# A decoder step's wkv stage: merge levels as one 64x64 matmul per head, and engine loops written out

## The reference, cut to what matters

```python
def step(S, inp):
    r_t, d_t, k_t, v_t, a_t, b_t = inp
    Sa = jnp.einsum('bhvk,bhk->bhv', S, a_t)
    S = S * d_t[:, :, None, :] + Sa[..., :, None] * b_t[..., None, :] + v_t[..., :, None] * k_t[..., None, :]
    return S, jnp.einsum('bhvk,bhk->bhv', S, r_t)
S, ys = lax.scan(step, S0, xs)
```

## Time and profile before

| | |
|---|---|
| median of 3 runs | 4897.39 us (4886.02 to 4908.73) |
| profiled execution, first to last instruction | 4900.2 us |
| mean granted TensorE clock | 0.914 |
| TensorE matmuls | busy 4308.0 us (88%) |
| VectorE | busy 2273.0 us (46%) |
| ScalarE | busy 1456.1 us (30%) |
| GpSimd | busy 1416.4 us (29%) |

### The profile page before, as it was taken

One profiled execution on the slowest core, in us unless ns is written; L12 is line 12 of the kernel. 1 busy time (PEld: TensorE's weight loads), 2 busy tenths in 40 slices (PEclk: granted clock), 3 DMA queues, 4 the chain that ended last, 5 costly groups with the idle time before them and its releaser, 6 DMA issues.

```text
span 4900.2 us, 72602 instructions
## 1 busy us (share of the span) xinstructions
PE 4308.0 (88%) x22425; PEld 3583.0 (73%) x22425; DVE 2273.0 (46%) x4969; ACT 1456.1 (30%) x2858; POOL 1416.4 (29%) x1222
## 2 busy tenths in 40 slices
PE   3789988998889989997989889997989787899996
PEld 3569866886679757885779667885879665678885
DVE  1246534545255535454266535444154553245554
ACT  1333233333333233333323233333322212022222
POOL 6232032443231123442331124442221011023331
PEclk9899998998889999998999899997998888699997
DMA  2320122332310112332310213332210112222221
GB/s 73 125 69 1 43 69 65 94 94 73 103 44 1 60 52 86 94 97 77 88 32 0 78 44 103 94 94 78 64 31 0 52 35 86 90 61 73 68 68 57
DMA packets 454929, 320.54 MB, mean 65 GB/s; under 512 B 18012, under 2 KB 420262, under 8 KB 453070
## 3 DMA queue, kind: packets, MB, share of 16 engines
q1 hardware_dynamic: 454758, 318.45, 21.1%
HBM read 296.99 MB, written 21.61 MB: 65 GB/s over the span
## 4 chain that ended last, share of the span: by engine, by line
PE 68%; DVE 15%; issue 9%; POOL 3%; ACT 3%; DMA 1%; DVEq 1%; ACTq 0%; POOLq 0%; SPq 0%
PE psum L671 66%; DVE xlo L1429 2%; PE psum L675 2%; POOL wlo L577 1%; DVE xT L1429 1%; DVE shifted L1429 1%; DVE zr L1432 1%; DVE ws L1429 1%; ACT whi L1102 1%; DVE shifted L1432 1%; DVE kkn_y L1429 1%; POOL stage L519 1%; DVE xT L1432 0%; DMA out_y_prompt<-zr 0%; ACT stage L1102 0%
## 5 line engine op out<-in xcount | busy, mean ns | idle before, releaser
L577 POOL TENSOR_TENSOR wlo<-wraw,whi 128x1024 fp32r<-128x1024 f32 x480 | 1152.3, 2401 | 2818.6 <-ACT whi L1102 2818.5
L671 PE MATMUL psum<-xhi,whi 128*128 128x512 f32 (+1 forms) x3136 | 1254.3, 400 | 58.5 <-DVE xlo L1429 41.1
L671 PE MATMUL psum<-xhi,wlo 128*128 128x512 f32 (+1 forms) x3136 | 1224.0, 390 | 0.0
L671 PE MATMUL psum<-xlo,whi 128*128 128x512 f32 (+1 forms) x3136 | 1224.0, 390 | 0.0
L1102 ACT ACTIVATE whi<-wraw 128x1024 fp32r<-128x1024 f32 x480 | 507.4, 1057 | 1226.2 <-PE psum L671 1161.4
L671 PEld LDWEIGHTS psum<-xhi,whi 128*128 128x128 f32 x3136 | 599.7, 191 | 231.6 <-DVE xlo L1429 81.1
L671 PEld LDWEIGHTS psum<-xhi,wlo 128*128 128x128 f32 x3136 | 599.7, 191 | 125.0
L671 PEld LDWEIGHTS psum<-xlo,whi 128*128 128x128 f32 x3136 | 601.2, 192 | 113.0 <-issue 1.4
L1429 DVE TENSOR_TENSOR xT<-xT,psum 128x512 f32<-128x512 f32 (+1 forms) x416 | 286.0, 688 | 246.0 <-PE psum L671 166.5
L1741 DVE TENSOR_SCALAR zr<-zr,fcw 128x512 f32<-128x512 f32 x176 | 91.9, 522 | 585.2 <-POOL fcarry L619 583.5
L671 PE MATMUL psum<-ws 128*128 128x64 f32 (+1 forms) x2560 | 350.7, 283 | 2.1 <-DVE ws L1595 1.7
(11 more groups left out here) (292 smaller groups left out, 5587.7 us busy)
## 6 DMA issues: line engine op xcount, KB each, us to landing
wraw<-in_w_up SPq DMA_DIRECT2D x176, 512.0 KB, 3.8
wraw<-in_w_in SPq DMA_DIRECT2D x104, 512.0 KB, 3.9
wraw<-in_w_down SPq DMA_DIRECT2D x88, 512.0 KB, 3.5
wraw<-in_w_out SPq DMA_DIRECT2D x32, 512.0 KB, 4.1
wraw<-in_wq SPq DMA_DIRECT2D x32, 512.0 KB, 4.0
wraw<-in_wo SPq DMA_DIRECT2D x32, 512.0 KB, 4.1
kkn_y<-in_x_prompt SPq DMA_DIRECT2D x4, 2048.0 KB, 9.3
xT_scratch<-xT SPq DMA_DIRECT2D x4, 2048.0 KB, 7.6
```

Of the source, the lines that this page charges most:

```text
L577: return e.tensor_tensor(wlo[i][:, :, :], wraw[i][:, :, :], whi[i][:, :, :].bitcast(F32), ALU.subtract).then_inc(lo_ready[i], 1)
L671: return e.matmul(out, lhsT, rhs, start=start, stop=stop)
```

## The change

1. In the merge levels each product of a pair of heads becomes two, one per head. The weights are the 64x64 diagonal block of the head, the moving side the head's 64 rows and 32 columns, and the result goes to the head's 64 partitions and its own 32 columns of the same bank. The parts of the bank that belong to neither head are no longer written; no copy uses them.
2. Every engine loop (blocks, projections, wkv, FFN and the others, on all engines) is written out as straight code, with constant waits and constant addresses. `LOOPS`, `Counts.loop`, `check_turn` and the increments of `passedA`, `passedG` and `passedV` go.

```diff
+                def per_head(bk, col, lhsT, rhs):
+                    n = 32 // rhs.shape[2]
+                    for h in range(2):
+                        a = slice(64 * h, 64 * h + 64)
+                        ins = mm(psum[a, bk, col + 32 * h:col + 32 * h + 32], lhsT[a, a], rhs[a, n * h:n * (h + 1), :])
+                    return ins
...
-                        mm(psum[:, bk, 0:64], TM[i][:, p, 384:512], half(QT[i][:, p, 0, :], m, 1)).then_inc(wk_mm[bk], 1)
+                        per_head(bk, 0, TM[i][:, p, 384:512], half(QT[i][:, p, 0, :], m, 1)).then_inc(wk_mm[bk], 1)
...
-                        ins = mm(psum[:, bk, 0:64], QT[i][:, p, 1, :], half(Zs[i][:, p, :], m, 1))
+                        ins = per_head(bk, 0, QT[i][:, p, 1, :], half(Zs[i][:, p, :], m, 1))
                         if l < len(MERGES) - 1:
-                            ins = mm(psum[:, bk, 64:128], Zs[i][:, p, :], half(QT[i][:, p, 1, :], m, 0))
+                            ins = per_head(bk, 64, Zs[i][:, p, :], half(QT[i][:, p, 1, :], m, 0))
...
-                with c.loop("wkv", NC // 2 - 1):
+                for _ in range(NC // 2 - 1):
                     wkv_pair()
...
-            with c.loop("block", NB - 1) as b:
+            for b in range(NB - 1):
                 one_block(b, False)
             one_block(NB - 1, True)
...
                 for l in range(1, len(MERGES)):
                     for i, p, bk in both:
                         e.wait_ge(wk_mm[bk], c(wk_mm[bk], 2))
-                        e.sem_inc(passedV, 1)
```

More of the change, by code:

```diff
@@ L1 @@
-from contextlib import ExitStack, contextmanager
+from contextlib import ExitStack
 import numpy as np
@@ L52 @@
 NLD = len(PAR) + 11
[L55 to L141, removed]
@@ L144, with __init__ @@
 class Counts:
-    def __init__(self, eng, name, passed=None):
-        self.eng, self.name, self.passed, self.n, self.turns = eng, name, passed, {}, []
+    def __init__(self):
+        self.n = {}
     def __call__(self, sem, k=1):
         v = self.n[sem.name] = self.n.get(sem.name, 0) + k
-        for i, per in self.turns:
-            if per.get(sem.name):
-                v = i * per[sem.name] + v
         return v
@@ L161, in skip @@
         self.n[sem.name] = self.n.get(sem.name, 0) + k
-    @contextmanager
-    def loop(self, label, count):
-        key = f"{self.name}.{label}"
-        per, before = LOOPS.get(key, {}), dict(self.n)
-        if self.passed is not None and self.turns:
-            self.eng.sem_inc(self.passed, 1)
-        with self.eng.Fori(0, count) as i:
-            self.turns.append((i, per))
-            yield i
-            self.turns.pop()
-        did = {s: v - before.get(s, 0) for s, v in self.n.items() if v != before.get(s, 0)}
-        check_turn(key, per, did)
-        for s, d in did.items():
-            self.n[s] = before.get(s, 0) + d * count
-def check_turn(key, per, did):
-    assert per == did, f"{key}: a turn asks for {did}"
 def hybrid_decoder_step(nc, I, O):
@@ L368, in _ @@
         def _(e):
-            c = Counts(e, "sync")
+            c = Counts()
             def slab(i, src, first=False):
@@ L419, in one_block @@
                 e.dma_start(xT_dram, xT[:, :, :].rearrange("p k t -> p (k t)")).then_inc(x_out, 16)
-                with c.loop("in", NIN // 2 - 1) as i:
+                for i in range(NIN // 2 - 1):
                     for j in range(2):
@@ L429, in one_block @@
                         sample_caches()
-                    with c.loop(name, KT // 2 - 1) as i:
+                    for i in range(KT // 2 - 1):
                         for j in range(2):
@@ L435, in one_block @@
                 ffn_up(0)
-                with c.loop("ffn", NF // 2 - 1) as i:
+                for i in range(NF // 2 - 1):
                     ffn_up(i + 1)
@@ L514, in _ @@
         def _(e):
-            c = Counts(e, "pool", passedG)
+            c = Counts()
             last = [0]
@@ L580, in splits @@
             def splits(label, pairs):
-                with c.loop(label, pairs):
+                for _ in range(pairs):
                     split(0)
@@ L609, in operands @@
                     e.wait_ge(qt_free, c(qt_free))
-                    e.sem_inc(passedG, 1)
                 unit(i)
@@ L639, in one_block @@
                 operands(1, C, True)
-                with c.loop("wkv", NC // 2 - 1) as j:
+                for j in range(NC // 2 - 1):
                     operands(0, j * (2 * C) + 2 * C)
@@ L667, in _ @@
         def _(e):
-            c = Counts(e, "pe")
+            c = Counts()
             def mm(out, lhsT, rhs, start=True, stop=True):
@@ L708, in phase @@
                 if pairs > 1:
-                    with c.loop(label + "s" * bool(sample), pairs - 1):
+                    for _ in range(pairs - 1):
                         dense(0, 0, sample, None, n)
@@ L937, in one_block @@
                 head_rows(8)
-                with c.loop("gates" + "s" * last, 4):
+                for _ in range(4):
                     dense(0, 0, s)
@@ L986, in one_block @@
                 ffn_up(s, tuple(range(KT)))
-                with c.loop("ffn" + "s" * last, NF // 2 - 1):
+                for _ in range(NF // 2 - 1):
                     ffn_up(s)
@@ L1098, in _ @@
         def _(e):
-            c = Counts(e, "act", passedA)
+            c = Counts()
             def act(out, src, func=ACT.Copy, **k):
@@ L1138, in _ @@
                 split_x(k, NMEM)
-            with c.loop("mem", 8):
+            for _ in range(8):
                 for j in range(2):
@@ L1174, in wkv_pair @@
                         e.wait_ge(wk_mm[bk], c(wk_mm[bk], 2))
-                        e.sem_inc(passedA, 1)
                         act(Y[:, p, bass.ds(t0 + i * C, C)], psum[:, bk, 0:C]).then_inc(wk_act[bk], 1)
             def residual(label):
-                with c.loop(label, KT // 2) as i:
+                for i in range(KT // 2):
                     for j in range(2):
@@ L1255, in one_block @@
                     split_x(k)
-                with c.loop("shift", NRW // 2) as i:
+                for i in range(NRW // 2):
                     for j in range(2):
@@ L1287, in one_block @@
                 gate_b(1)
-                with c.loop("gate_c", 2) as i:
+                for i in range(2):
                     for j in range(2):
                         e.wait_ge(slab_done[j], c(slab_done[j]))
-                        e.sem_inc(passedA, 1)
                         act(cb[:, bass.ds(2 * i + j, 1), 2:TB + 2].rearrange("p a t -> p (a t)"), psum[:, j, :]).then_inc(ach, 1)
@@ L1296, in one_block @@
                         split_w(j)
-                with c.loop("h_in", 2):
+                for _ in range(2):
                     for j in range(2):
@@ L1313, in one_block @@
                 dec_chunk(1)
-                with c.loop("wkv", NC // 2 - 1) as i:
+                for i in range(NC // 2 - 1):
                     wkv_pair(i * (2 * C), 2 * i + 2)
@@ L1331, in one_block @@
                     split_x(k)
-                with c.loop("q", KT // 2) as i:
+                for i in range(KT // 2):
                     for j in range(2):
                         e.wait_ge(slab_done[j], c(slab_done[j]))
-                        e.sem_inc(passedA, 1)
                         act(q_sb[:, bass.ds(2 * i + j, 1), :].rearrange("p a t -> p (a t)"), psum[:, j, :]).then_inc(ach, 1)
@@ L1352, in one_block @@
                 ffn_hidden()
-                with c.loop("ffn" + "s" * last, NF // 2 - 1) as i:
+                for i in range(NF // 2 - 1):
                     ffn_up(i + 1)
@@ L1425, in _ @@
         def _(e):
-            c = Counts(e, "dve", passedV)
+            c = Counts()
             def tt(out, a, b, op=ALU.mult):
@@ L1556, in _ @@
             lo(before, NMEM)
-            with c.loop("mem", 8) as i:
+            for i in range(8):
                 for j in range(2):
@@ L1644, in residual @@
                 acc_start()
-                with c.loop(label + "s" * last, KT // 2) as i:
+                for i in range(KT // 2):
                     for j in range(2):
@@ L1830, in sample_out @@
                         e.sem_inc(free[4 + j], 1)
-                with c.loop("shift" + "s" * last, NRW // 2) as i:
+                for i in range(NRW // 2):
                     for j in range(2):
@@ L1879, in one_block @@
                     e.wait_ge(vch, c(vch))
-                with c.loop("gate_c" + "s" * last, 2) as i:
+                for i in range(2):
                     for j in range(2):
@@ L1884, in one_block @@
                 e.wait_ge(a2v, c(a2v, 4))
-                with c.loop("h_in" + "s" * last, 2) as i:
+                for i in range(2):
                     for j in range(2):
@@ L1980, in one_block @@
                 normalise("norm_x")
-                with c.loop("q" + "s" * last, KT // 2) as i:
+                for i in range(KT // 2):
                     for j in range(2):
```

11 lines of the change are left out of this document (removed).

## The result

The changed kernel takes 4696.43 us (4680.06 to 4706.37, 4 runs) against 4900.91 us for the kernel before: ratio 0.9579, 95% interval 0.9553 to 0.9605. That is 204 us less, inside the range given, but two and a half times the 81 us of the sum, and nearly the price of the rival in which the clock stays high (4677). That nearness is chance: half of the merges lost the clock, and the loops gave the rest. The profiled execution has a span of 4700.4 us, 199.8 less than before.

A forecast was written before the change was run, and what follows sets the result against it. TensorE was taken to bound the kernel (busy 4308.0 of 4900.2 us, 68% of the chain). 4900.2 - 45 - 36 = 4819, or 4816 us on the runs' median; range 4675 to 4960, the forecast's own 4745 to 4885.

The forecast's parts named there:

- the 81 us of the sum: Whole kernel: forecast saving, 45 us from the per-head merge products and 36 us from the written-out loops.
- the rival in which the clock stays high: Merges overlap the heads and stay at 2.4 GHz: products give -184 us, total 4677 on the median; chance 0.26.
- Prices of a product: wkv merges: two heads side by side cost 108 ns at 2.4 GHz and 213 ns at 1.2 GHz, against 224 before at 2.4.
- no gain: Merge products no cheaper (27 ns dispatch, or levels otherwise as long); only written-out loops help, some 4861 us; chance 0.14.
- no overlap: Merges: heads sharing a bank run one after the other and the clock falls, 5236 us, or 5046 with half overlap; chance 0.14.
- I take a quarter of a pair's merges high, three quarters low: wkv merges: 0.25 x 15.0 + 0.75 x 23.9 = 21.7 us per pair, since the clock was expected to fall in most.
- the 2 us of the final stage: Behind each pair's merges: time added while the clock comes back, taken as 2 us, between 0 and 7.3.
- Part 2: -36 us: All engines' loops written out: 19 us saved in the wkv stage plus 17 us elsewhere; ends 0 and -100.
- part 1: wkv merges: one product per head, 424 us falling to 379 over 16 pairs, -45 us; all low -10, all high -184.
- The 19 us counted for the wkv stage's stretches: wkv stage: loop work off the chain, 1.2 us per pair, 19 us in 16 pairs.
- The 17 us for all the rest: Outside the wkv stage: half of what remains of the chain's 1% "DVEq", about 49 us, after some 15 for wkv.
- Nothing in fetching the longer code: Instruction transfers, perhaps 6.3 MB more: cost counted as 0; the rival of late fetching, up to +100 us, had chance 0.04.

## Why the prediction was wrong

The direction and most of the mechanism were right; two terms of the sum were too small, and together they make nearly all of the 123 us that are missing.

**Prices of a product: right.** 108 ns at 2.4 GHz (105 to 115 in the profile) and 213 at 1.2 were forecast; 117 and 213 came. The merges of a pair were to take 15.0 and 23.9 us; they take 14.4 to 14.9 and 22.3 to 23.8. Eight instructions go out in 117 ns, 15 ns apart, so the 27 ns of the earlier trace rows were no floor. The rivals of no gain and of no overlap fall with the same two levels. VectorE, which the prediction named as next to be late, isn't late: from 429.27 to 442.0 its merge copies still wait for TensorE, 3.3 us in all. The Trainium skill ("TensorEngine Tiling (Array Packing)", Restrictions and Gotchas) says that different row tiles can't access one PSUM bank at once. What the prediction drew from that, one head after the other, isn't borne out here: the two heads use both row halves and one bank, and their 8 products take 0.93 us where one after the other would take 1.7. Whether both write the bank at the same instant isn't shown: four streams of 64 columns in turn would take 4 x 27 = 108 ns, an estimate from the 54 ns of a load with its 128 columns, and would fit into 117.

**"I take a quarter of a pair's merges high, three quarters low": mis-sized.** Half of the pairs stayed high throughout, in the profiled execution. The mean of the 16 is 18.8 us, not 21.7, and the 2 us of the final stage is paid by 8 pairs, not 16: some -110 us (-126 and 16 back) for -45. The price of a low final stage itself held: the stretch between merges, 24.2 to 24.8 us after a high pair, is 26.0 to 27.1 after a low one. One row behind the step was misread. The 10.24 us at 0.50 from 284.85 on the earlier trace rows were to show that matmuls on half the rows leave the clock low:

```profile
284.69 7.07 PE L671 MATMUL psum<-zr,lora_wa 64*128 64x512 f32 x8
291.68 0.79 PE L671 MATMUL psum<-xhi,whi 128*128 128x512 f32 x1
```

Only the first 7 us are of that kind, and the matmuls on all rows behind them ran at 0.50 too. The 47.8 us for the low pair are likewise the stretch at 0.50, which runs into the final stage; from its first to its last merge product it took 45.7. That is only 2 us off. The step treated the two parts as independent. With the other engines' loops in place 11 of 16 pairs fall, and the total was -47.5, next to the -45 forecast; with the loops written out 8 fall. Why those and not others isn't settled: that TensorE waits less for VectorE is the obvious reading, but no run changed that alone.

**"Part 2: -36 us": mis-sized, by a factor of two and a half.** Alone it gave -115. Some 23 us of that are the clock of the one low pair, which the prediction counts in part 1; the loops gave the other 92, inside the end of -100 that the prediction allowed. The 19 us counted for the wkv stage's stretches were right (-17, 2 of them from that pair). The 17 us for all the rest were not: -77. The count went by the chain's 1% of "DVEq", halved, with none of the 9% of "issue" beside it. The chain shows more per step of VectorE: a register instruction and its "issue", 0.11 us of the 0.95 from one addition to the next. The kernel's own table had the number of such steps: in `LOOPS`, `dve.block` raises `vch` 517 times in a turn. Three looped blocks are 1551; at half of 0.11 us each, 85 us, near the 77. This is an estimate after the fact, and the half, for steps that TensorE hides, is assumed and not measured.

**Nothing in fetching the longer code:** 2 MB more of instructions, and the merges keep TensorE busy for 14.99 of 15.04 us. That shows it for the merges; elsewhere no run tests it apart from the loops' gain.

## What to carry to other kernels

A wait on a count that a loop has to work out costs its engine register instructions. Where the engine stands on the chain with many short dependent steps, as VectorE does here, it pays to write its loops out; the engine to choose is better found by writing out one engine's loops than by the chain's share of "issue". When a matmul is cut into smaller ones, ask whether the stretch keeps its clock: a busy TensorE doesn't say so, and two kinds of the same stage in one trace do. Where the moving columns don't set the pace, leave them wide: here they were free and kept 2.4 GHz. And when two kernels are compared, count first how many of such stretches each trace has at the low clock: one pair was worth 23 us of a difference that looked like the loops'.

## What the runs showed of the hardware

Two 64-row halves of the array working on results in one PSUM bank, at different partitions, overlap: 117 ns at 2.4 GHz and 213 at 1.2 for four passes, where one half after the other would take 216 and an estimated 427. Moving 64 columns instead of 32 costs nothing behind these loads (0.94 us for eight products against 0.93). With 32 columns 8 of 16 merge stretches fell to 1.2 GHz though TensorE was busy in all of them; with 64 in a third of the products, none did. Where the clock fell, it fell 1.6 to 4.5 us after the first merge product, in the kernel before too (3.2 us, one pair in 16, with 64 columns moved over all 128 rows). A register instruction ahead of a wait adds 0.11 us to a dependent step of VectorE (0.95 for 0.84); one that runs while the engine works doesn't show on the chain.
